# Splitting six more weight tiles in layer 1, and finishing the last expert by halves of the width, in a two-layer decoder kernel

## The reference, cut to what matters

```
for i in range(2):
    h = rmsnorm(x, norm_mix[i])
    z = h @ w_in[i]               # [SSM input 512 | q,k,v 3x768 | memory q 512 | gates 3x1024]
    y_ssm = ssm_branch(z[..., :512], ...) @ w_ssm_out[i]    # complex diagonal scan over time
    y_att = dilated_attention(q, k, v, ...) @ w_att_out[i]  # QK-norm and rotary on q and k
    y_mem = memory_attention(mq, rmsnorm(mem) @ w_mem_kv[i], ...) @ w_mem_out[i]
    x = x + (gated sum of the three branches) @ w_o[i]
    h2 = rmsnorm(x, norm_ffn[i])
    x = x + (swiglu(h2) if i == 0 else moe_swiglu(h2))      # sum over experts of gate * expert(h2)
```

## Time and profile before

| what | value |
|---|---|
| median of the runs | 1843.31 us |
| profiled execution | 1846.5 us |
| its span | 1844.8 us |
| granted TensorE clock, mean | 0.991 |
| TensorE busy | 1797.5 us (97%) |
| VectorE busy | 1451.0 us (79%) |
| ScalarE busy | 1126.7 us (61%) |
| GpSimd busy | 82.1 us (4%) |

### The profile page before, as it was taken

How to read it: one execution, slowest core, us unless ns; L and a number is a source line. 1 busy time by engine, 2 the same in 40 slices (tenths; PEclk the granted TensorE clock), 3 DMA queues, 4 the chain that set the end, 5 groups by cost and what they waited for, 6 DMA issues and landing times.

```text
span 1844.8 us, 22446 instructions
## 1 busy us (share of the span) xinstructions
PE 1797.5 (97%) x8075; PEld 1397.3 (76%) x8075; DVE 1451.0 (79%) x1280; ACT 1126.7 (61%) x1208; POOL 82.1 (4%) x115
## 2 busy tenths in 40 slices
PE   7999999999999999998999999999999999999997
PEld 5446878888874468887888878888878888888886
DVE  7996546676836865467889898898888988988986
ACT  5336463654351374636776776777777767777774
POOL 1123000100001310000000000000000000000000
PEclk9999999999999999998999999999999999999998
DMA  7334434765443343376999999999999999999994
GB/s 226 116 116 134 137 115 159 223 204 184 161 152 121 114 137 115 114 245 212 366 372 355 356 353 331 373 359 349 365 344 370 367 340 367 355 378 373 352 371 163
DMA packets 227343, 477.01 MB, mean 259 GB/s; under 512 B 15996, under 2 KB 40696, under 8 KB 227256
## 3 DMA queue, kind: packets, MB, share of 16 engines
q1 hardware_dynamic: 226872, 474.99, 72.9%
q0 software_dynamic: 288, 0.79, 0.2%
q10 hardware_dynamic: 96, 0.02, 0.0%
HBM read 474.71 MB, written 1.05 MB: 258 GB/s over the span
## 4 chain that ended last, share of the span: by engine, by line
PE 92%; DVE 3%; ACT 2%; issue 1%; SPq 1%; DMA 1%; ACTq 0%; DVEq 0%
PE ps L610 25%; PE ps L612 24%; PE ps L611 24%; PE ps L645 9%; PE ps L1033 1%; PE ps L811 1%; PE ps L783 1%; PE ps L1011 1%; PE ps L731 1%; PE ps L744 1%; DVE t L1863 1%; ACT hi L1415 1%; PE ps L598 1%; PE ps L794 1%; DMA ring<-in_w_mem_kv 1%
## 5 line engine op out<-in xcount | busy, mean ns | idle before, releaser
L2013 DVE TENSOR_TENSOR lo<-ring_e,hi 128x2048 fp32r<-128x2048 f32 x336 | 767.5, 2290 | 103.0 <-ACT hi L1415 102.7
L1415 ACT ACTIVATE hi<-ring_e 128x2048 fp32r<-128x2048 f32 x336 | 644.1, 1918 | 183.0 <-PE ps L612 182.5
L610 PE MATMUL ps<-hi,xe_hi 128*128 128x512 f32 x896 | 356.0, 397 | 6.0 <-issue 5.5
L612 PE MATMUL ps<-hi,xe_lo 128*128 128x512 f32 x896 | 350.0, 391 | 0.0
L611 PE MATMUL ps<-lo,xe_hi 128*128 128x512 f32 x896 | 350.0, 391 | 0.0
L610 PEld LDWEIGHTS ps<-hi,xe_hi 128*128 128x128 f32 x896 | 168.5, 188 | 42.9 <-issue 6.7
L645 PE MATMUL ps<-ring,hT 128*128 128x512 f32 x448 | 198.3, 597 | 0.0
L612 PEld LDWEIGHTS ps<-hi,xe_lo 128*128 128x128 f32 x896 | 168.7, 188 | 36.5
L611 PEld LDWEIGHTS ps<-lo,xe_hi 128*128 128x128 f32 x896 | 168.9, 189 | 33.2
L610 PE MATMUL ps<-hi,aT_hi 128*128 128x512 f32 x464 | 181.6, 391 | 0.0
L612 PE MATMUL ps<-hi,aT_lo 128*128 128x512 f32 x464 | 180.8, 390 | 0.0
(11 more groups left out here) (357 smaller groups left out, 2314.6 us busy)
## 6 DMA issues: line engine op xcount, KB each, us to landing
ring_e<-in_moe_w_gate SPq DMA_DIRECT2D x112, 1024.0 KB, 7.1
ring_e<-in_moe_w_up SPq DMA_DIRECT2D x112, 1024.0 KB, 7.1
ring_e<-in_moe_w_down SPq DMA_DIRECT2D x112, 1024.0 KB, 6.8
ring<-in_w_in SPq DMA_DIRECT2D x50, 1024.0 KB, 5.1
ring<-in_ffn_w_gate SPq DMA_DIRECT2D x22, 512.0 KB, 4.1
ring<-in_ffn_w_up SPq DMA_DIRECT2D x22, 512.0 KB, 5.1
ring<-in_ffn_w_down SPq DMA_DIRECT2D x11, 1024.0 KB, 5.0
ring<-in_w_mem_kv SPq DMA_DIRECT2D x8, 1024.0 KB, 5.2
```

What stands on the lines that cost most here:

```text
L610: nc.tensor.matmul(o, x_hi, w_hi, start=first, stop=False, skip_group_check=True)
L612: return nc.tensor.matmul(o, x_lo, w_hi, start=False, stop=end, skip_group_check=True)
L1415: nc.scalar.activation(hi[:, m % H, :], src, ACT.Copy).then_inc(sem("hi_ready"), 1)
L2013: last = V.tensor_tensor(lo[:, m % H, :], src, hi[:, m % H, :].bitcast(F32), ALU.subtract)
```

## The change

Three things are altered; layer 0 keeps its plain tiles.

1. **Layer 1, input split early.** Right after the transposed input `hT` is complete, ScalarE rounds it to `x_early` (in columns of `z` that are not yet in use) and VectorE forms `xT_lo` from it, in another place than before. A second rounded copy, `xT_hi`, is made after block 1; the one before tile 18 goes.
2. **Layer 1, tiles 4, 5, 6, 7, 16 and 17 are split.** ScalarE and VectorE get six more pairs of instructions, at places written into their orders. The squares of the memory keys move from behind block 5 to ahead of block 0.
3. **The last expert by halves.** `y_hi`, `y_lo`, the spreading products and the additions go by halves of the width, each half is stored by a DMA of its own as soon as its two additions are done, and the read of the count and the jump come behind the stores.

The diff, cut to these parts, in the order TensorE, ScalarE, VectorE, and then the end (SyncE, ScalarE, VectorE):

```
-                columns(n, 2, (hT,), KT)
+                early = (hT,)
+                if l > 0:
+                    pe.wait_ge(sem("early_input_ready"), 1)
+                    early = (x_early, xT_lo)
+                columns(n, 2, early, KT)
...
-                part(n + 2, 0, 2, (hT,), KT)
+                part(n + 2, 0, 2, early, KT)
...
-                part(n + 2, 1, 2, (hT,), KT)
+                part(n + 2, 1, 2, early, KT)
...
-                columns(n_in + 2 * SSM_COLS, 2, (hT,), KT)
+                columns(n_in + 2 * SSM_COLS, 2, (hT,) if l == 0 else xT, KT)
...
+                    act.wait_ge(sem("transposed_used"), batches_to(l, "h"))
+                    nc.scalar.activation(x_early.rearrange("p k t -> p (k t)"), flat(hT), ACT.Copy).then_inc(
+                        sem("early_hi_ready"), 1)
+                    weights_high(l)
...
                 if l > 0:
+                    weights_high(l)
                     tables(l)
+                    weights_high(l)
+                    act.wait_ge(sem("columns_used"), cols[0])
+                    head_squares(kv, 0, XD, XH, lambda c, hd: rm[:, 1, c, hd:hd + 1],
+                                 lambda c, hd: xT_hi[:, XH + hd, c * XD:(c + 1) * XD]).then_inc(sem("mk_squared"), 1)
                 act.wait_ge(sem("x_rs"), 2 * l + 1)
                 take_columns(z[:, :, 0:BANK])
+                if l > 0:
+                    weights_high(l)
...
                 take_columns(z[:, :, BANK:2 * BANK])
+                if l > 0:
+                    act.wait_ge(sem("mk_squared"), l + 1)
+                    nc.scalar.activation(flat(xT_hi), flat(hT), ACT.Copy).then_inc(sem("input_hi_ready"), 1)
...
                     take_columns(z[:, :, n * BANK:(n + 1) * BANK])
+                    if l > 0 and n == SSM_COLS - 1:
+                        weights_high(l)
...
+                    if l > 0 and n == SSM_COLS - 2:
+                        act.wait_ge(sem("qk_squared"), l + 1)
+                        weights_high(l)
...
+                    dve.wait_ge(sem("early_hi_ready"), 1)
+                    V.tensor_tensor(xT_lo[:], hT[:], x_early.bitcast(F32), ALU.subtract).then_inc(
+                        sem("early_input_ready"), 1)
+                    weights_low(l, 4)
...
+                    if l > 0 and v == NJ // 2 - 2:
+                        weights_low(l)
                 skip_path(l, KS - 1)
+                if l > 0:
+                    weights_low(l)
...
+            for half in range(2):
+                o = slice(half * BANK, (half + 1) * BANK)
+                sp.wait_ge(sem("added"), 4 * (NE - 1) + 3 + 2 * half)
+                sp.dma_start(rows_out[:, :, o], x[:, :, o]).then_inc(sem("stored"), 16)
             sp.wait_ge(sem("routed"), 1)
             busiest = sp.value_load(most[0:1, 0:1])
...
-            sp.wait_ge(sem("x_final"), 1)
-            sp.dma_start(out[0].rearrange("(c p) d -> p c d", p=P), x[:]).then_inc(sem("stored"), 16)
...
+                            if halves and i == 1 and half == 1:
+                                last.then_inc(sem("y_half_done"), 1)
...
+                        act.wait_ge(sem("y_half_done"), e // NE + 1)
+                        nc.scalar.activation(y_hi[:, 0:BANK], ps[:, 4, :], ACT.Copy).then_inc(sem("y_half_hi_ready"), 1)
...
+                        dve.wait_ge(sem("y_half_hi_ready"), e // NE + 1)
+                        V.tensor_tensor(y_lo[:, 0:BANK], y[:, 0:BANK], y_hi[:, 0:BANK].bitcast(F32),
+                                        ALU.subtract).then_inc(sem("y_half_ready"), 1)
```

More of the change, by code:

```diff
@@ L102, in decoder_trunk @@
         h_hi = renamed("h_hi", [P, C, D], F32R)
+        xT_lo = renamed("xT_lo", [P, KD, SEQ], F32R)
         h = sb("h", [P, C, D])
-        xT_lo = renamed("xT_lo", [P, KD, SEQ], F32R)
+        merged = renamed("merged", [P, C, D], F32)
         hT = sb("hT", [P, KD, SEQ])
@@ L141, in decoder_trunk @@
         hi_m = mb("hi_m", [P, 2, TILE], F32R)
+        z_rounded = renamed("z_rounded", [P, C, COLS], F32R)
         z = mb("z", [P, C, COLS])
@@ L1034, in act_transposes, with down @@
                     last.then_inc(sem("actT_done"), 1)
-                def down(a, m, shift, first, end, between=None, lhs=(aT_hi, aT_lo)):
+                def down(a, m, shift, first, end, between=None, lhs=(aT_hi, aT_lo), halves=False):
                     pe.wait_ge(sem("actT_ready"), a)
@@ L1095, in expert @@
                     pe.wait_ge(sem("dispatchT_ready"), e + 1)
-                    pe.wait_ge(sem("y_ready"), e + 1)
-                    for c in range(C):
-                        t = slice(c * P, (c + 1) * P)
-                        for half in range(2):
-                            o = ps[:, ADD_BANKS[2 * c + half], :]
-                            d = slice(half * BANK, (half + 1) * BANK)
-                            nc.tensor.matmul(o, dispT[:, t], y_hi[:, d], start=True, stop=False)
-                            nc.tensor.matmul(o, dispT[:, t], y_lo[:, d], start=False, stop=True).then_inc(
-                                sem("combined"), 1)
+                    for c, half in ADD_BY_HALVES if last_one else ADD_BY_ROWS:
+                        if (c, half) == (0, 0) and last_one:
+                            pe.wait_ge(sem("y_half_ready"), e // NE + 1)
+                        elif c == 0 and half == (1 if last_one else 0):
+                            pe.wait_ge(sem("y_ready"), e + 1)
+                        t = slice(c * P, (c + 1) * P)
+                        o = ps[:, ADD_BANKS[2 * c + half], :]
+                        d = slice(half * BANK, (half + 1) * BANK)
+                        nc.tensor.matmul(o, dispT[:, t], y_hi[:, d], start=True, stop=False)
+                        nc.tensor.matmul(o, dispT[:, t], y_lo[:, d], start=False, stop=True).then_inc(
+                            sem("combined"), 1)
                 def one_pass(pair0):
@@ L1242, in input_transposed, with head_squares @@
                         from_batch(pairs(hT, q, lambda k: gains[:, 0, l, k:k + 1]))
+                def head_squares(src, o, dim, heads, sums, scrap):
+                    act.wait_ge(sem("columns_used"), cols[0])
+                    for c in range(C):
+                        for hd in range(heads):
+                            last = nc.scalar.activation(scrap(c, hd), src[:, c, o + hd * dim:o + (hd + 1) * dim],
+                                                        ACT.Square, accum_out=sums(c, hd))
+                    return last
                 if l > 0:
@@ L1282, in mixer @@
                 take_columns(z[:, :, BANK:2 * BANK])
-                def head_squares(src, o, dim, heads, sums, scrap):
-                    act.wait_ge(sem("columns_used"), cols[0])
-                    for c in range(C):
-                        for hd in range(heads):
-                            last = nc.scalar.activation(scrap(c, hd), src[:, c, o + hd * dim:o + (hd + 1) * dim],
-                                                        ACT.Square, accum_out=sums(c, hd))
-                    return last
+                if l > 0:
+                    act.wait_ge(sem("mk_squared"), l + 1)
+                    nc.scalar.activation(flat(xT_hi), flat(hT), ACT.Copy).then_inc(sem("input_hi_ready"), 1)
                 for n in range(2, SSM_COLS + 1):
```

76 lines of the change are left out of this document (48 added, 28 removed).

## The result

The changed kernel took 1850.19 us (median of 18 runs, 1843.98 to 1857.06). The kernel before took 1843.91 us beside it (18 runs, 1842.37 to 1846.39). The ratio is 1.003, with a 95% interval of 1.0024 to 1.0036: slower by 4.4 to 6.6 us. I had forecast 1844.0 us and "the same", so some 6 us are missing in my sum.

A forecast was written before the change was run, and what follows sets the result against it. TensorE, busy for 97% of the span, was taken to bound the kernel. +6.7 us in layer 1 and -6.0 at the end gave +0.7, hence 1847.2 by the profile and 1844.0 us as median, range 1838.5 to 1849.

The forecast's parts named there:

- The sum: Whole kernel: +6.7 us in layer 1 and -6.0 at the end make +0.7 us, forecast 1844.0 us.
- Parts 1 and 2: Layer 1: split tiles 4 to 7 give a 0.3 us lead; the scan and tile 16 leave tile 18 6.7 us late.
- C: Rival, layer 1: GpSimd's roots block VectorE at the SBUF port; tile 18 at +12, total +6, 1849 us; chance 0.05.
- D: Rival, layer 1: TensorE stays at 1.2 GHz through tiles 16 and 17; layer 1 +12.4, total +6.4, 1849.7 us; chance 0.15.
- SyncE's jump: End: moved behind the stores, beside the transfer; would set the end if it takes over 2.9 us.
- Layer 1: From the split tiles through the scan to tile 18's start: +6.7 us, bounds for the scan stretch +4 and +9.
- wait before block 0: Front of layer 1's scan: TensorE waits 4.9 us for ScalarE, and a likely clock fall costs 1.6 us.
- lead into the scan: Layer 1: TensorE enters the scan 0.3 us early, bounds 0 and 1.9.
- Step 7: Layer 1's scan: VectorE waits for tile 16's copy and rest, so this step starts 9.2 us later, less the lead.
- The end: Last expert by halves with two overlapping stores and the jump behind them: -6.0 us, bounds 4.5 and 6.5.
- A: Rival, front: TensorE keeps 2.4 GHz after 4.9 us idle; lead 1.9, layer 1 costs 5.1, 1842.4 us; chance 0.17.
- B: Rival, scan: tile 16's copy is there when step 6 ends; layer 1 -0.2, total -6.2, 1837.1 us; chance 0.13.

The follow-up runs named there:

- e9: Kernel before with 97 instructions of fulfilled waits, one after each of layer 0's first 97 plain products on TensorE; 1849.18 us, ratio 1.0028.
- e10: Changed kernel with 159 instructions of fulfilled waits spread over layer 0's plain products on TensorE; 1846.01 us, ratio to before 1.0011.
- e5: Kernel before with TensorE's loop over the first three expert pairs written out; 1835.05 us, ratio 0.9947.
- e6: Changed kernel with TensorE's loop over the first three expert pairs written out; 1838.84 us, ratio to before 0.9965.
- e1: Kernel before with only the last expert by halves and two stores added; 1837.84 us against 1844.07, ratio 0.9964.
- e3: Kernel before with 194 fulfilled waits (97 instructions) added at the start of TensorE's program; 1853.23 us (+9.2).
- e2: Changed kernel without the last expert by halves, its end as before; 1854.6 us, ratio to before 1.0059.
- e4: Changed kernel with 318 fulfilled waits (159 instructions) added at the start of TensorE's program; 1860.41 us (+16.3).
- e7: Changed kernel with VectorE forming tile 16's rest behind scan step 7 instead of before it; 1845.74 us, 1.001 of before.
- e11: As e7, but VectorE also waits for GpSimd's join of step 7 before it forms the rest; 1849.26 us in one profile.
- e8: Changed kernel with e7's edit, TensorE's loop written out, and block 0 taken ahead of the memory keys' squares; 1831.81 us, ratio to before 0.9932.
- e12: e8 with tiles 16 and 17 copied together, memory keys' roots before the scan, key scaling behind the copies, rotary products before the last skip product; 1829.12 us.

## Why the prediction was wrong

**The step that failed is "The sum": "+6.7 in layer 1, -6.0 at the end: +0.7 us".** It has no term for the first seven experts, whose work the change doesn't touch. Parts 1 and 2 counted the products of split tiles by their time alone and not as instructions: 96 more, and a wait. They move the loop over expert pairs against the packets in which TensorE's program arrives, and that costs 4.4 us (252.76 - 248.33 in the column of the loop): shown by e9 without any of the change's work, taken away by e10, and absent in e5 and e6. Of the 5.6 us by which the sum was short (+0.7 against +6.3), 4.4 are this one. None of the rivals had it; the nearest in time, C and D, gave 1849 and 1849.7 for reasons that didn't occur.

The Trainium skill, Runtime: NRT & Kernel Launch, section "Instruction fetch mechanics", says that a taken branch outside the fetched window waits for its target's page of 256 instructions. The traces bear this out for TensorE's long loop, by the packet 2.6 us ahead of each restart. I had weighed that rule on SyncE's jump alone and not on TensorE's, which the profile of the kernel before showed as waits of 3.25 and 2.24 us named "issue". Weighing it there would still have priced both kernels alike, since both make the same jumps: what differs is the second wait, and that was learned only from the runs.

**Layer 1** was sized well: five profiles with the old layer 1 (before, e1, e3, e5, e9) have 333.3 us in the column "front" on average, five with the new one (changed, e2, e4, e6, e10) 340.3, +7.0 against +6.7. By its steps: the wait before block 0 was 4.5 us (4.9 forecast), with the fall of the clock (0.53 over 7 us); but the lead into the scan of 0.3 us was a lag of 0.5 at block 4. Step 7 came 9.7 us late (8.9 with the lead). The delay went through whole by step 7, join, roots and key scaling. Savings on tiles 16 and 17 were worth nothing, as written: TensorE was through with them and waited again, 1.88, 0.94 and 0.37 us, before the last transposes.

**The end** was -5.5 us (128.3 to 122.8) by the profiles and -6.2 by e1's median, against -6.0. With 7.0 and 4.4 that makes +5.9; measured were +6.3. That layer 1 and the end came so near the forecast is in part luck: each column varies by more than they are off.

**The rivals.** A: the clock did fall in front. B: VectorE did wait. D: the clock was low from 647.9 us on, through the product of step 7's states and the first seven products of tile 16, and back at 2.4 GHz from 654.6 on, so tile 18 wasn't held up. C, the lock at SBUF, did not delay anything in the changed kernel: tile 17's rest took its usual 2.28 us and the eight products with `rgain` their 1.17 beside the 8.03 us of roots. But I read too much into that. The Trainium skill, SBUF — State Buffer, section "SBUF: two separate sides", says that the later of such two instructions stands still for the other, and for GpSimd's join and scaling that is what e7 and e11 show (3.24 for 1.27 us, 2.34 for 0.24). Only the roots, 8.04 us long, held up nobody. One row had refuted the rule for one kind of instruction, not for its neighbours.

Not settled in full: why the medians of e5 and e6 differ by 3.8 us where the means of front and end give 1.5. Their own two profiles give 4.0 (8.6 in front, -4.6 at the end), and both columns vary by 1 to 3 us among kernels whose code there is the same. The granted clock goes with much of that:

- In front, all profiles share a long low stretch just before the first gather. Apart from it, with the old layer 1, e1 and e5 (332.2 us) have no low clock at tile 18 or later; before (333.9, at 666.7 us) and e3 (333.3, at 778.1) have one low stretch there, e9 (334.9) has two. With the new layer 1, the changed kernel and e10 (339.7 and 340.0) have none there, e4 and e6 (341.0 and 340.8) have one, and so has e2 (339.9), whose fall before block 0 was a shorter one (0.76 over 7 us). Like against like, layer 1 costs 7.5 us rather than 7.0.
- At the end, the eight spreading products met the low clock in before, e2 and e3 (0.60, 0.58 and 0.51; 128.7 to 128.9 us) and not in e5 and e9 (1.00; 127.3 and 127.6).

So the profile of e6 has a low stretch in front that e5's has not, and e5's lacks the one at the end, too. What sets whether the clock falls isn't shown: before tile 18 the waits are the same in all five, within 0.01 us. The column of the loop covers 6.6 of the 9.2 us that e5's median gains. Nor did I try other places for the loop.

## What to carry to other kernels

Count what an edit adds to an engine's instruction stream ahead of a long runtime loop (here of some 1,800 instructions; the short one inside it cost nothing). A wait named "issue" at the start of a round was here program code on its way; its cost depends on where the loop stands, may change by several microseconds with an edit hundreds of microseconds away, and goes when the loop is written out on that engine alone. Before work is given to an engine with idle time, find which instruction stands behind it in its queue: what was lost here lay in the order (squares, copy, rest, step), and moving the rest of tile 16 behind step 7 won 3.3 of the 7.5 us back.

## What the runs showed of the hardware

- A restart of TensorE's loop over expert pairs stood still for 2.1 to 3.3 us before its first product, and in the six kernels with the unlucky place for up to 3.38 us more behind the twelfth; with the low clock behind it two restarts cost 5.3 to 13.6 us (the column of the loop, less 241.3).
- A loop of some 1,800 instructions (by the count in the program) was fetched anew in every round: there are 62 packets with the loop (63 in e4 and e10), 57 with its three rounds written out; code kept between the rounds would have made the first number much the smaller. A loop of 76 products inside it ran its three rounds without a packet for 59 us and without a wait.
- An instruction that waits for two fulfilled semaphores took TensorE 0.108 us where nothing hid it, and nothing measurable between products of 0.86 us (the first 100 recorded matmuls of them took 53.03 us in before and in e9).
- GpSimd's joins and scalings stood still while VectorE formed a rest from two inputs in SBUF (2.28 us; the join took 3.24 us for 1.27, the scaling 2.34 for 0.24); in e12 VectorE's rest took 2.78 us when it began during a join. GpSimd's roots of 8.04 us held up nothing.
- TensorE kept 2.4 GHz with 2.19 us of idleness (e8, e12) and fell to 1.2 GHz with 4.52 us (seven kernels), at the same place of the program. Before tile 18, waits of 1.17 and 0.46 us went with a fall in before and e9 and with none in e1, e3 and e5: the length of a wait alone doesn't tell.
